# A hybrid attention and state-space layer: order of VectorE's work in two places, and a last tile without a copy

## What is computed

```python
u = rms_norm(hid, norm_pre_w)
proj = jnp.einsum('bsd,de->bse', u, w_in)          # 6672 columns: q, k, v, g, z, xbc, dt
q, k, v, g_attn, z, xbc, dt_raw = jnp.split(proj, ...)
attn = mixture_of_dilations(q, k, v) * silu(g_attn)  # windows (128,1), (512,4), (2048,16)
xbc = silu(causal_depthwise_conv(xbc, conv_w, conv_b))
y = ssd_chunked(xs, dt, a, b_mat, c_mat) + d_skip * xs   # chunks of 128 tokens, state carried on
y = gated_group_rms_norm(y, z, ssm_norm_w)
out = jnp.einsum('bse,ed->bsd', concatenate([attn, y]), w_out)   # 2048 -> 1024
return hid + rms_norm(out, norm_post_w)
```

## Time and profile before

| | |
|---|---|
| median of 3 runs | 2234.01 us (2233.54 to 2239.61) |
| the profiled execution: its own time | 2234.33 us |
| its span, first to last instruction | 2232.6 us |
| granted PE clock, mean over the span | 0.983 |
| busy: PE, DVE, ACT, POOL | 96%, 61%, 46%, 65% |

### The profile page before, as it was taken

One profiled execution on the slowest core, in us unless ns is written; L12 is line 12 of the kernel. 1 busy time (PEld: TensorE's weight loads), 2 busy tenths in 40 slices (PEclk: granted clock), 3 DMA queues, 4 the chain that ended last, 5 costly groups with the idle time before them and its releaser, 6 DMA issues. The chain is left out here.

```text
span 2232.6 us, 34835 instructions
## 1 busy us (share of the span) xinstructions
PE 2147.4 (96%) x12057; PEld 1828.9 (82%) x12057; DVE 1357.0 (61%) x2579; ACT 1036.2 (46%) x2397; POOL 1445.6 (65%) x880
## 2 busy tenths in 40 slices
PE   6999999999999999999989999999997699999998
PEld 4778888888888888888869999999996478888886
DVE  7555666344656665233467777777776767666661
ACT  5324443343434433334348777777776322332231
POOL 5778888778688888777625565654643355655552
PEclk9999999999999999999989999999998799999999
DMA  4552334334533333333445656556557244434331
GB/s 142 201 179 86 113 104 132 101 102 137 190 104 105 115 117 109 102 106 101 126 108 127 153 143 149 116 136 162 134 155 250 77 136 141 137 129 137 127 102 57
DMA packets 260221, 287.20 MB, mean 129 GB/s; under 512 B 78420, under 2 KB 228112, under 8 KB 251984
## 3 DMA queue, kind: packets, MB, share of 16 engines
q1 hardware_dynamic: 258944, 277.50, 41.7%
q0 software_dynamic: 1104, 7.47, 0.8%
HBM read 195.28 MB, written 81.00 MB: 124 GB/s over the span
## 5 line engine op out<-in xcount | busy, mean ns | idle before, releaser
L993 PE MATMUL mm<-b_hi,w_hi 128*128 128x512 f32 x1456 | 572.6, 393 | 7.6 <-ACT c L638 6.2
L995 PE MATMUL mm<-b_hi,w_lo 128*128 128x512 f32 x1456 | 568.5, 390 | 0.0
L994 PE MATMUL mm<-b_lo,w_hi 128*128 128x512 f32 x1456 | 568.1, 390 | 0.0
L544 POOL TENSOR_TENSOR w_lo<-w_raw,w_hi 128x512 fp32r<-128x512 f32 x208 | 298.1, 1441 | 79.9 <-ACT w_hi L618 72.2
L993 PEld LDWEIGHTS mm<-b_hi,w_hi 128*128 128x128 f32 x1456 | 274.2, 188 | 64.5 <-issue 9.1
L995 PEld LDWEIGHTS mm<-b_hi,w_lo 128*128 128x128 f32 x1456 | 274.1, 188 | 57.5
L994 PEld LDWEIGHTS mm<-b_lo,w_hi 128*128 128x128 f32 x1456 | 274.3, 188 | 55.6
L618 ACT ACTIVATE w_hi<-w_raw 128x512 fp32r<-128x512 f32 x208 | 130.7, 629 | 254.6 <-PE mm L995 233.8
L1823 PE MATMUL ps_t<-ident_b,probs 128*128 128x128 f32 x1136 | 214.4, 279 | 12.1 <-ACT probs L1743 10.7
L818 DVE SCALAR_TENSOR_TENSOR fm<-mm,u 128x512 f32<-128x512 f32 x120 | 92.1, 769 | 187.9 <-PE mm L995 187.9
L2389 PE MATMUL ps_out<-wo_hi,mix_hi 128*128 128x512 f32 x480 | 194.0, 404 | 1.3 <-ACT mix_hi L2295 1.3
(11 more groups left out here) (255 smaller groups left out, 4470.2 us busy)
## 6 DMA issues: line engine op xcount, KB each, us to landing
w_raw<-in_w_in_dram SPq DMA_DIRECT2D x52, 1024.0 KB, 5.1
feat<-fm SPq DMA_DIRECT2D x56, 512.0 KB, 5.3
tok<-tok_tile SPq DMA_DIRECT2D x52, 512.0 KB, 3.5
raw_q<-feat SPq DMA_DIRECT2D x32, 512.0 KB, 5.9
raw_k<-feat SPq DMA_DIRECT2D x32, 512.0 KB, 6.3
cum_b<-cum_scratch SPq DMA_DIRECT2D x16, 1024.0 KB, 7.3
cls_nat<-cls_out SPq DMA_DIRECT2D x64, 132.0 KB, 2.7
v_cls<-tok SPq DMA_DIRECT2D x64, 128.0 KB, 3.6
```

Source lines behind the costliest of these rows:

```text
L544: pool.tensor_tensor(wl[o][:, :, :], source(o, n), wh[o][:, :, :].bitcast(F32), ALU.subtract)\
L993: pe.matmul(bank, w_hi[:, k, :], bh[o][:, k, :], start=(opens and k == 0), stop=False)
L994: pe.matmul(bank, w_hi[:, k, :], bl[o][:, k, :], start=False, stop=False)
L995: last = pe.matmul(bank, w_lo[:, k, :], bh[o][:, k, :], start=False, stop=(closes and k == KH - 1))
```

## The change

It has three parts. In the input projection the four differences of a group stand together behind the read of S2, instead of one each behind four reads. At the start of the scan the low output weights are made in another order, PE takes the high scan weights of chunk 0 for both halves in one run and the low ones later, and chunk 2's decay is made as chunk 1's, on ACT. In the last tile ACT squares the banks without a copy, DVE makes the mean, scales from the banks and adds the residual by halves, and each half has a store of its own.

```diff
-                def late_sum(j, i):
+                def late_sums(j):
...
-                    if i == 0:
-                        dve.wait_ge(normed, HT + 2 * j + 2)
-                    else:
-                        dve.wait_ge(sums_late, 4 * j + i)
-                    dst, one, other = ((t1, u12, u11), (t2, u22, t1), (t3, u22, u12), (t4, u21, t2))[i]
-                    dve.tensor_tensor(dst, one, other, ALU.subtract).then_inc(sums_late, 1)
+                    dve.wait_ge(normed, HT + 2 * j + 2)
+                    dve.tensor_tensor(t1, u12, u11, ALU.subtract).then_inc(sums_late, 1)
+                    dve.tensor_tensor(t3, u22, u12, ALU.subtract).then_inc(sums_late, 1)
+                    dve.wait_ge(sums_late, 4 * j + 1)
+                    dve.tensor_tensor(t2, u22, t1, ALU.subtract).then_inc(sums_late, 1)
+                    dve.wait_ge(sums_late, 4 * j + 3)
+                    dve.tensor_tensor(t4, u21, t2, ALU.subtract).then_inc(sums_late, 1)
...
                     read(s, S2, u2[:, :], c1[:, :])
                     if n in PREP:
-                        late_sum(PREP[n], 0)
+                        late_sums(PREP[n])
...
-                    wait(sp, "seg_made", c if c < 1 else SSM_HEADS if c == 1 else 2 * SSM_HEADS + c - 2)
+                    wait(sp, "seg_made", SSM_HEADS * min(c, 3) + max(c - 3, 0))
...
-                store(LAST)
-                sp.wait_ge(S["stored"], 16 * CHUNKS)
+                for h in range(2):
+                    half = slice(h * BANK, (h + 1) * BANK)
+                    sp.wait_ge(S["out_added"], CHUNKS + h)
+                    sp.dma_start(out[tokens(LAST), half], o_tok[:, half]).then_inc(S["stored"], 16)
+                sp.wait_ge(S["stored"], 16 * (CHUNKS + 1))
...
-                out_root(LAST)
-                add_residual(LAST)
+                pool.wait_ge(S["out_mean"], 2 * CHUNKS)
+                pool.tensor_tensor(rstd[:, 2:3], mean[:, 3:4], minus_half[:, 2:3], ALU.pow).then_inc(S["out_rstd"], 1)
...
+                def last_out():
+
+                    dve.wait_ge(S["out_squared"], 2 * CHUNKS)
+                    dve.wait_ge(S["out_mean"], 2 * LAST)
+                    dve.wait_ge(S["out_rstd"], LAST)
+                    dve.tensor_tensor(mean[:, 2:3], ssq[:, 2:3], ssq[:, 3:4], ALU.add).then_inc(S["out_mean"], 1)
+                    dve.wait_ge(S["out_mean"], 2 * LAST + 1)
+                    dve.tensor_scalar(mean[:, 3:4], mean[:, 2:3], 1.0 / D_MODEL, EPS, ALU.mult, ALU.add)\
+                       .then_inc(S["out_mean"], 1)
+                    dve.wait_ge(S["out_rstd"], CHUNKS)
...
+                    for h in range(2):
+                        half = slice(h * BANK, (h + 1) * BANK)
+                        dve.scalar_tensor_tensor(out=o_tok[:, half], in0=ps_out[h][:, :], scalar=rstd[:, 2:3],
+                                                 in1=post_w[:, half], op0=ALU.mult, op1=ALU.mult)\
+                           .then_inc(S["out_scaled"], 1)
+                        dve.wait_ge(S["out_scaled"], 2 * LAST + h + 1)
+                        dve.tensor_tensor(o_tok[:, half], o_tok[:, half], x_res[:, half], ALU.add).then_inc(S["out_added"], 1)
...
                 weigh(0)
+                take_low(range(0, 2))
                 new_state(0)
-                take_low(range(0, 2))
+                take_low(range(2, 4))
                 diag_and_gate(0)
                 small_exponents(1)
-                take_low(range(2, 5))
+                take_low(range(4, KA))
                 weigh(1)
                 off_and_skip(1)
                 mix_low(0)
-                take_low(range(5, 9))
                 new_state(1)
+                take_low(range(KA, KA + 1))
                 for c in range(1, CHUNKS):
                     diag_and_gate(c)
-                    if c == 1:
-                        take_low(range(9, 12))
                     if c < LAST:
                         small_exponents(c + 1)
-                        segments(c + 1)
+                        if c >= 2:
+                            segments(c + 1)
                     if c == 1:
-                        take_low(range(12, KO))
+                        take_low(range(KA + 1, KO))
...
                 take_high(PORTION[3])
+                early_segments(2, range(0, SSM_HEADS // 2))
                 for c in range(1, CHUNKS):
                     square_y(c)
                     if c < LAST:
                         grow(c + 1)
+                    if c == 1:
+                        early_segments(2, range(SSM_HEADS // 2, SSM_HEADS))
                     scale_y(c)
-                    if c < LAST:
+                    if c == 1:
+                        early_decay(2)
+                    elif c < LAST:
                         exp_decay(c + 1)
...
                 for h in range(2):
-                    out_read(LAST, h)
+                    act.wait_ge(S["out_done"], 2 * LAST + h + 1)
+                    act.wait_ge(S["out_mean"], 2 * LAST)
+                    act.activation(z2[:, h * BANK:(h + 1) * BANK], ps_out[h][:, :], ACT.Square,
+                                   accum_out=ssq[:, 2 + h:3 + h]).then_inc(S["out_squared"], 1)
...
                 chunk_states(1)
-                for c in range(1, CHUNKS):
+                diagonal(1)
+                first_scan()
+                turn(1)
+                mix_b_and_c(2)
+                read_state(2)
+                last_weights_low(0)
+                last_weights_low(1)
+                chunk_states(2)
+                for c in range(2, CHUNKS):
```

More of the change, by code:

```diff
@@ L2314, in _ @@
                 take_high(PORTION[1])
[L2315 removed]
+                early_segments(1, range(0, SSM_HEADS // 2))
                 square_y(0)
                 grow(1)
[L2318 removed]
+                early_segments(1, range(SSM_HEADS // 2, SSM_HEADS))
                 scale_y(0)
[L2320 removed]
+                early_decay(1)
                 y_high(0)
@@ L2372, in first_scan, with last_weights_low @@
                         pe.wait_ge(S["wo_hi_made"], kk + 1)
-                        pe.matmul(ps_out[h][:, :], mix_hi[:, kk, :], wo_hi[:, kk, cols_h], start=False, stop=False)
-                        pe.matmul(ps_out[h][:, :], mix_lo[:, kk, :], wo_hi[:, kk, cols_h], start=False, stop=False)
+                        for h in range(2):
+                            cols_h = slice(h * BANK, (h + 1) * BANK)
+                            pe.matmul(ps_out[h][:, :], mix_hi[:, kk, :], wo_hi[:, kk, cols_h], start=False, stop=False)
+                            pe.matmul(ps_out[h][:, :], mix_lo[:, kk, :], wo_hi[:, kk, cols_h], start=False, stop=False)
+                def last_weights_low(h):
                     for kk in range(KA, KO):
                         pe.wait_ge(S["wo_lo_made"], kk + 1)
-                        last = pe.matmul(ps_out[h][:, :], mix_hi[:, kk, :], wo_lo[kk][:, cols_h], start=False, stop=(kk == KO - 1))
+                        last = pe.matmul(ps_out[h][:, :], mix_hi[:, kk, :], wo_lo[kk][:, h * BANK:(h + 1) * BANK],
+                                         start=False, stop=(kk == KO - 1))
                     last.then_inc(S["out_done"], 1)
```

41 lines of the change are left out of this document (17 added, 24 removed).

## The result

| | before | changed |
|---|---|---|
| median, in one series | 2235.18 us (2233.54 to 2239.61, 4 runs) | 2215.47 us (2215.14 to 2216.83, 4 runs) |
| ratio, 95% interval | | 0.991 (0.9893 to 0.9927) |
| profiled execution, span | 2232.6 us | 2215.1 us |
| granted PE clock, mean | 0.983 | 0.988 |

The kernel became 0.9% faster, by 19.7 us between the medians and 17.5 between the spans. The forecast was 31.3 us; 2215.5 lies above its range.

What follows compares the result with a forecast made beforehand. PE was taken as the bound in the long stretches, with gains only where it stands still or runs at the lower clock: 7.9 + 21.5 + 1.9 = 31.3 us off 2234.3 gave 2203.0 us, range 2198 to 2213.

Steps and rivals of the forecast that it cites:

- Part 1, 7.9 us forecast: Input projection: differences made together remove PE's stalls of 1.80 and 4.38 us ahead of S1 and 1.7 of low clock.
- the price of the differences: Input projection, DVE: differences in a row start every 1.1 us, so the last begins 3.3 us after the first, not 6.5.
- The slack is 0.6 us only; if it is missed, PE waits some tenths: Input projection, step 3: DVE's A12 read done at 129.5, PE needing it for S4 at 130.1.
- part 1 is given back: Rival, input projection: earlier issue of loads may not land earlier, or A12's slack is missed; 2207 to 2211 us, chance 0.12.
- Part 2, 21.5 us forecast: Start of the scan: with DVE as the chain, diagonal(2) starts at 1759.6 instead of 1781.1.
- The rival on the clock: Start of the scan: PE's clock low from 1736 on, gain 12 us instead of 21.5, 2212 to 2213 in all; chance 0.12.
- the seven tiles meet the same two operations of POOL, so I charge it once: Start of the scan: a 1.9 us loss of tiles beside POOL, already inside DVE's 28.28 us, not added again.
- its 1.9: Start of the scan: 1.9 us added for the weighing of chunk 2's decay meeting POOL's fading of the state.
- PE is not the limit: Start of the scan: PE's work, 17 us at full clock and 20 with margin, ends at 1756 when started at 1735.6.
- both halves of the weighing are blocked: Rival, start of the scan: POOL stops both instructions, gain 20.0 to 18 us, 2204.5 to 2206.5; 0.2 of the forecast's chance.
- Part 3, 1.9 us forecast: Last tile: 0.49 without the copy, 1.0 in scaling and adding, 0.4 from a last store of half the bytes.
- the slower rival: Chunk loop: DVE later against PE in each of 14 chunks; 3 us a chunk give 2245 us; chance 0.03.

Runs made afterwards that it cites:

- low_waits: The changed kernel, with POOL in steps 0 to 3 making the next low weights only after the four differences are through; 2206.53 us, ratio 0.9866.
- p23: The changed kernel with the four differences put back in their old order; 2216.49 us, 0.9915 of the kernel before.
- reordered: The changed kernel with the last two low-weight tiles made after chunk 2's skip and their four matmuls behind diagonal(2); 2218.68 us, ratio 0.9933.
- pool_late: The changed kernel with POOL starting chunk 2's skip, and so its fading, only when all low-weight tiles are made; 2219.04 us, ratio 0.9926.
- filled: The changed kernel with matmuls repeated in PE's idle places around chunk 1, results unchanged; 2214.55 us, ratio 0.9902.
- p3_only: The kernel before with only the last-tile change; 2233.09 us, ratio 0.9985.
- p1_low_waits: The kernel before with the four differences together and POOL's low weights waiting for them; 2226.73 us, ratio 0.9959.

## Why the prediction failed, step by step

**Part 1, 7.9 us forecast: about 1 measured, within the noise.** The step that failed is the price of the differences: "A difference lasts 1.18, and a successor starts 0.1 before the end that is recorded, so in a row they start every 1.1 us and the last begins 3.3 us after the first." Beside POOL's reads they start every 1.7. DVE's and POOL's timelines of the kernel before in step 0, which the prediction did not use, show what the 1.18 was:

```profile
67.65 1.18 DVE L810 TENSOR_TENSOR conv_in<-tok_tile,conv_in 128x512 f32<-128x512 f32 x1
68.75 0.68 DVE L818 SCALAR_TENSOR_TENSOR u<-mm,u 128x512 f32<-128x512 f32 x1
69.35 1.18 DVE L810 TENSOR_TENSOR conv_in<-tok_tile 128x512 f32<-128x512 f32 x1
...
68.36 3.33 POOL L544 TENSOR_TENSOR w_lo<-w_raw,w_hi 128x512 fp32r<-128x512 f32 x2
```

From difference to difference it is 1.70 there too, with a read of a PSUM bank between them, and POOL's two take 1.66 each. So 1.18 was not the length of a difference (that is 0.68) but of a difference that waits for its turn; the bank's read of 0.6 us lay in the time that POOL's instruction needed anyway. Moving the reads away freed next to nothing and put A12's read 6.2 us behind the start of the first difference. The loads of the three following groups, which the prediction had 1.8, 5.0 and 8.2 us sooner, were issued at 78.94, 101.04 and 121.77 instead of 78.19, 100.40 and 124.09: two of them later (by the 0.8 us that this execution was late with from the start), the third 2.3 us sooner. (The rows beside these repeat the pattern through all of step 0.) In steps 1 to 3 the old order has, beside this, the wait for the store of `fm`.

The prediction did weigh this rule, on part 2 alone. The Trainium skill, page "SBUF — State Buffer", section "Who interferes with whom", says that a DVE instruction with two SBUF inputs contends with a GpSimd instruction that reads SBUF and not with one that only writes, and that one with at most one SBUF input does not contend, outside the modes of DVE that use two ports. By that rule the trace agrees at each point: 0.68 for a bank's read beside POOL, 1.7 for a difference beside POOL's reads, 0.68 beside POOL's writes.

The rest of part 1 stood. "The slack is 0.6 us only; if it is missed, PE waits some tenths" named the place of the new wait; it was missed by 1.5 to 2.7 us. From the first difference to A12's read it took 6.2 instead of 4.5, which is 1.7 of it. The rest is that DVE's read of S2, with the loads no sooner, came late against PE: in step 3 it began 5.1 us before S4 was due, where the forecast had 6.3. That a gain is handed on from group to group held in low_waits: its loads are issued at 73.50, 94.14 and 112.52, so 4.7, 6.3 and 11.6 us sooner, and with them all waits and the low clock are gone. The rival "part 1 is given back" came true for part 1, but not by its first reason: from the stores' issue to the next load it took 5.9, 7.3 and 5.9 us in the changed kernel and 5.9, 5.9 and 7.5 before, so over the three groups the transfers took nothing back.

The 7.9 itself is less well founded than low_waits makes it look. It is the sum of what PE lost in one execution of the kernel before, and that was the least of the four with the old order; a gain that is large enough removes whatever there is. Against the mean of the four the scan of low_waits starts 10 us sooner, not 8.2. And its differences follow each other 0.6 us apart, not the 1.1 that the forecast used.

**Part 2, 21.5 us forecast: 16.6 measured.** The mechanism held: the wait for the low weights is gone, and from diagonal(1) on DVE sets the pace up to its last step. Chunk 2's decay on ACT did not hold PE in the changed kernel; in p23 and reordered PE waited 0.4 us for ACT ahead of turn(1), time that the low weights hid. Four sizes were off, and add up to the missing 4.9:

- Diagonal(1) started 1.1 us later than forecast, 32.0 us after `read_state(0)` instead of 30.8. The four attention tiles ahead of it, beside POOL, took 1.6 each.
- DVE waited 0.8 us for diagonal(1), which took 5.50 us at the low clock. The rival on the clock had this place right; it came for 6.8 us, not for the whole stretch.
- The seven tiles and the weighing took 13.39 + 2.36. "the seven tiles meet the same two operations of POOL, so I charge it once": they met three, the last of them the fading that the prediction had beside the weighing, and lost some 5 us against a quiet 1.2 each, while the weighing lost nothing and its 1.9 were charged for naught. Net 1.5 us. The decay's second pass, too, seems to have had a loss beside POOL in its 2.81, since for the next chunk it takes 1.23 in the changed kernel, from 1775.14; with the pass gone from this place, the tiles met POOL instead. pool_late shows that the loss only changes its place.
- "PE is not the limit" failed for the last 1.5 us. After a wait of 2.34 for the last tile, the nine matmuls that stood behind it ran at the low clock, and the state products stood behind them. The sum of PE's work was right; its last matmuls could not start before the last tile. filled shows the 1.5 us gone when the clock stays up.

The forecast's own rival, that both halves of the weighing are blocked, did not come for chunk 2 (2.36 us); chunk 1's, at 5.25, was nearly as slow before (4.88).

**Part 3, 1.9 us forecast: 2.3 in the trace**, 2.7 in the time of p3_only. Its terms held: a half is scaled in 0.75 and added in 0.69, 2.9 us in all. Of the 2.3, 0.7 lie ahead of the scaling (0.49 forecast), 1.0 in scaling and adding (1.0), and 0.6 behind the last addition (0.4).

**The loop** ran without a gap, as forecast; the slower rival did not come.

**The sum**: 31.3 forecast, less 4.9 in part 2, plus 0.4 in part 3, is 26.8; the spans differ by 17.5. The remaining 9.3 lie ahead of the scan: the 7.9 that part 1 did not bring and 1.4 by which the changed kernel's scan even starts later. Of these 1.4, 0.8 were there before the first difference in this execution; the waits of step 3 vary between executions, and I did not separate that further. With POOL's wait added, the kernel is at 2206.5, and the span of low_waits, 2204.4, is 28.2 below that of the kernel before: 8.2 ahead of the scan, 17.8 up to diagonal(2), 2.2 at the end.

## What to carry to other kernels

Before an instruction is priced by its row, look at what the other engine is doing in the same microsecond: if its starts keep the other's pace, its length is a turn and not a cost, and what stands between two turns is free and gains nothing by being moved. Where two engines share something, the repair may be a wait on the one that has a step to spare: here one wait on POOL turned a reordering worth about 1 us into one of about 9 (0.9959 for p1_low_waits, 6 to 12 us by its interval). And where PE waits and then has work in front of the next handover, price that work at the clock it will have after the wait.

## What the runs showed of the hardware that I had not expected

- DVE's 512-column difference with two SBUF inputs takes 0.68 us alone and starts 0.60 after its predecessor; beside POOL instructions that read SBUF it takes 1.77 and starts 1.70 after it, while POOL's go from 1.29 to 1.66. Neither stops for several instructions: in these rows they alternate one for one. Beside POOL's memsets of the same tiles it stayed at 0.68.
- More idle time can cost more than it frees. In pool_late a handover that came 1.6 us sooner met a PE that had waited 3.05 us, and the same 32 matmuls took 7.06 instead of 3.68 at the low clock. In reordered a wait of 1.35 stood ahead of 13.7 us of low clock. In filled, with matmuls that compute nothing new in the idle places, the clock stayed at 1.00 from 1722 to 1765, where it had been low twice.
